# Three paddings in a TensorE-bound two-block kernel: split-precision operands start at a multiple of 256 bytes in place of 64 past it

## The reference

```python
def first_block(x, ...):
    xn = rmsnorm(h, norm1_w)
    qd, kd, vd, qc, kc, vc, gd, gc = split(xn @ w_in)
    o_d = diff_attention(qd, kd, vd, ...)        # 8 heads, two maps, a1 - lam * a2, rmsnorm
    o_c = chunk_attention(qc, kc, vc, rel_bias)  # 8 heads
    merged = sigmoid(gd + b) * (o_d @ w_branch_diff) + sigmoid(gc + b) * (o_c @ w_branch_chunk)
    h = h + merged @ w_out
    h = h + peer(rmsnorm(h, norm2_w), peer_wq, keys, u, v)   # 16,384 one-neuron experts
    return rmsnorm(h, final_norm_w)

def second_block(x, ...):
    x = x + 0.5 * rms_norm(swiglu(rms_norm(x, g1), w_gu1, w_down1), g2)
    x = x + rms_norm(hybrid_mixer(rms_norm(x, g3), ...), g4)  # conv, linear recurrence, window attention
    x = x + 0.5 * rms_norm(swiglu(rms_norm(x, g5), w_gu2, w_down2), g6)
    return x
```

## The kernel before

| tensors | before | after |
|---|---|---|
| `wh`, `wl`, `raw`, `resid` | 128 | 128 |
| `xh`, `xl`, `wb`, `wcol` | 64 | 0 |
| `rt`, `dg`, `ones`, `ident`, `iota`, `nd`, `i1T`, `i2T`, `iota8`, `gT` | 224 | 160 |
| the small ones from `ssq` to `lsg` | 0 to 224 | each 64 lower |
| `odh`, `odl`, `och`, `ocl` | 64 | 0 |
| `y`, `gate`, `oc`, `ah`, `al`, `fh`, `fl`, `oh`, `ol`, `gst`, `one2`, `g2` | 128 | 128 |
| `qkT`, `vd`, `vc`, `rb` | 64 | 64 |

## Time and profile before

### The profile page before, as it was taken

How to read it: one execution, slowest core, us unless ns; L and a number is a source line. 1 busy time by engine, 2 the same in 40 slices (tenths; PEclk the granted TensorE clock), 3 DMA queues, 4 the chain that set the end, 5 groups by cost and what they waited for, 6 DMA issues and landing times.

```text
span 1505.2 us, 26993 instructions
## 1 busy us (share of the span) xinstructions
PE 1484.6 (99%) x10806; PEld 1371.5 (91%) x10806; DVE 1064.7 (71%) x1581; ACT 730.3 (49%) x853; POOL 310.3 (21%) x306
## 2 busy tenths in 40 slices
PE   8999999999999999998999999999999999999998
PEld 8989998999999999997888888888999888899986
DVE  6657676699999999845555555566877577787753
ACT  5366654545454554544444444445444457754441
POOL 3000000011100111126666667760000010000000
PEclk9999999999999999999999999999999999999999
DMA  8643354577666678887888888875555553355552
GB/s 311 203 152 138 129 173 168 185 244 245 230 228 211 216 254 278 285 302 271 290 287 288 289 289 291 290 278 187 191 196 197 195 183 119 131 181 192 190 194 80
DMA packets 56697, 329.76 MB, mean 219 GB/s; under 512 B 7536, under 2 KB 7584, under 8 KB 25232
## 3 DMA queue, kind: packets, MB, share of 16 engines
q1 hardware_dynamic: 36288, 259.01, 50.3%
q0 software_dynamic: 20304, 69.21, 12.6%
HBM read 294.64 MB, written 33.55 MB: 218 GB/s over the span
## 4 chain that ended last, share of the span: by engine, by line
PE 96%; DVE 2%; ACT 1%; issue 1%; DMA 0%; DVEq 0%; ACTq 0%
PE ub L1909 18%; PE ub L1911 17%; PE ub L1910 17%; PE acc L1909 11%; PE acc L1911 11%; PE acc L1910 11%; PE acc L2151 3%; PE acc L2022 1%; PE mb L2046 1%; PE mb L1911 1%; PE mb L1910 1%; PE mb L1909 1%; PE mb L2032 0%; PE acc L2126 0%; DMA resid<-in_x 0%
## 5 line engine op out<-in xcount | busy, mean ns | idle before, releaser
L963 DVE TENSOR_TENSOR wl<-raw,wh 128x2048 fp32r<-128x2048 f32 x244 | 560.3, 2299 | 203.2 <-ACT wh L555 137.9
L1909 PE MATMUL ub<-xh,wh 128*128 128x256 f32 x2168 | 608.8, 281 | 1.7 <-DVE wl L1189 0.8
L1911 PE MATMUL ub<-xh,wl 128*128 128x256 f32 x2168 | 601.0, 277 | 0.0
L1910 PE MATMUL ub<-xl,wh 128*128 128x256 f32 x2168 | 601.0, 277 | 0.0
L1909 PEld LDWEIGHTS ub<-xh,wh 128*128 128x128 f32 x2168 | 407.3, 188 | 10.2 <-issue 6.1
L1910 PEld LDWEIGHTS ub<-xl,wh 128*128 128x128 f32 x2168 | 408.8, 189 | 0.1
L555 ACT CAST wh<-raw 128x2048 fp32r<-128x2048 f32 x184 | 351.0, 1909 | 116.3 <-DMA raw<-in_wstream 116.0
L1911 PEld LDWEIGHTS ub<-xh,wl 128*128 128x128 f32 x2168 | 407.1, 188 | 0.0
L1909 PE MATMUL acc<-wh,ah 128*128 128x512 f32 x512 | 200.6, 392 | 3.9 <-issue 3.9
L1910 PE MATMUL acc<-wl,ah 128*128 128x512 f32 x512 | 200.2, 391 | 0.0
L1911 PE MATMUL acc<-wh,al 128*128 128x512 f32 x512 | 200.1, 391 | 0.0
(11 more groups left out here) (377 smaller groups left out, 1765.2 us busy)
## 6 DMA issues: line engine op xcount, KB each, us to landing
raw<-in_wstream SPq DMA_DIRECT2D x244, 1024.0 KB, 4.9
gates<-gst POOLq DMA_DIRECT2D x16, 1024.0 KB, 14.7
gl_in<-gates POOLq DMA_DIRECT2D x64, 256.0 KB, 3.7
hidden<-hid POOLq DMA_DIRECT2D x60, 256.0 KB, 4.9
hid<-hidden POOLq DMA_DIRECT2D x60, 256.0 KB, 3.6
resid<-in_x SPq DMA_DIRECT2D x2, 512.0 KB, 4.1
rb<-in_rel POOLq DMA_DIRECT2D x1, 1024.0 KB, 6.0
wb<-in_ffn_post_g POOLq DMA_DIRECT2D x2, 512.0 KB, 5.2
```

Of the source, the lines that this page charges most:

```text
L963: v.tensor_tensor(wl[:, slot, :], raw[:, slot, :], wh[:, slot, :].bitcast(F32), ALU.subtract).then_inc(w_low, 1)
L1909: pe.matmul(dst, sh, mh, start=first, stop=False)
L1910: pe.matmul(dst, sh, ml, start=False, stop=False)
L1911: return pe.matmul(dst, sl, mh, start=False, stop=last)
```

## The change

The first unused tensor shrinks by 64 bytes, and the second grows by as much; between the two everything starts 64 bytes lower, and behind the second nothing moves. The third, ahead of `odh`, shrinks by 64 bytes; nothing but `odh`, `odl`, `och` and `ocl` lies behind it on its stack.

```diff
@@ build_program
         resid = sb("resid", [P, TT, D])
-        sb("shift_x", [P, 48])
+        sb("shift_x", [P, 32])
         xh = sb("xh", [P, KD, T], F32R)
         xl = sb("xl", [P, KD, T], F32R)
...
         lsg = sb("lsg", [P, 6, LT])
-        sb("shift_y", [P, 48])
+        sb("shift_y", [P, 64])
...
-        sb("shift_o", [P, 24], at=st2)
+        sb("shift_o", [P, 8], at=st2)
         odh = sb("odh", [P, KD, T], F32R, at=st2)
```

## The result

| | before | after |
|---|---|---|
| median, us | 1506.2 (4 runs, 1503.15 to 1509.45) | 1530.5 (4 runs, 1530.06 to 1531.09) |
| ratio | | 1.0145, 95% interval 1.0123 to 1.0168 |
| span of the traced execution, us | 1505.2 | 1528.9 |

One execution of the kernel before, among 14 in the series beside the first experiments, took 3006.4 us in a slow state and is left out of the ratios.

The account below looks back on a forecast made before the run. TensorE, busy 99% of the span, was taken as the bound: matmul count times spacing. All four terms were taken as 0 on the profiled 1506.85 us, which stands 0.25 us under the median, giving 1507.1 us; range 1499 to 1531 us.

Parts of the forecast that it names:

- the rivals at both ends: Matmul spacing in units: only the short rhythm, 1499.7 us, 15%; the longer one in all units, 1530.3 us, 20%.
- The bound and the readings: TensorE busy 99% of the span; time is matmul count times spacing; chunks with ah, al stationary stay at 226.7 ns.
- Two rhythms, chosen by breaks: 256-column units run at 113.3 or 117.8 ns, a break in the stream choosing; the longer costs 6.8 us now.
- part 1: xh, xl moving at 0 against wh, wl at 128, 6,648 matmuls: taken as 0, bounds -6.8 and +23.2 us.
- Part 2: odh, odl, och, ocl, 288 more matmuls of the same kind: 1.3 us at most, taken as 0.
- Part 3: xh, xl as stationary operands, 288 matmuls at 2.2 ns: between -0.6 and +0.6 us, taken as 0.
- Part 4: ident, dg, rt, wb, wcol and small tensors, mostly hidden behind TensorE: 0.4 us either way, taken as 0.
- the longer rhythm in all units: Rival for the units, L1909 to L1911: every spacing in the longer rhythm, +23.2 us, 1530.3 us; chance 20%.
- only the short rhythm: Rival: at 128 bytes' distance the reads never meet in the costly way, -7.4 us, 1499.7 us; chance 15%.
- The rule weighed: TensorE's moving and weight reads use independent ports, so every term is 0 and the time 1507.1 us.

Follow-up runs that it names:

- rest_only: Against the kernel before: xh and xl stay at 64, all else that the change moved is 64 bytes lower modulo 256; 1508.4 us (10 runs), ratio 1.0019.
- x_at_128: Against the kernel before: xh and xl start at 128 modulo 256, as wh and wl do, all else unmoved; 1534.1 us (4 runs), ratio 1.0166.

## Why the prediction was wrong

The forecast was 1507.1 us, no change; 1530.5 was measured. That this lies inside the stated range of 1499 to 1531 us says little, since the range had been drawn around the rivals at both ends.

- **The bound and the readings** held: 99% busy, the loss is all in spacings, the other engines don't show in it, the chunks without moved operands stayed at 226.7 ns.
- **Two rhythms, chosen by breaks** held at the old distance and is now shown for the breaks by transposes, by moving one and by 16 changes of rhythm in 16. Its size (4.45 ns, 6.8 us in that trace) was right.
- **The step that failed is the choice in part 1** to carry both rhythms over to a distance of 128 bytes, because they occur at 64. No row bore on it, as the text says itself; "most natural" stood in for a row. The runs show that each distance has its own set: at -64 and 64 two rhythms with the short one among them, at 128 and at 0 none at 113.3. The term put at 0 measured +28.8 us (114.47 to 118.91 ns).
- **Part 2** was sized right (up to 1.3 us; 1.3 us measured), its taken value of 0 wrong for the same reason. **Part 3** went over its upper end: 1.0 us for +0.6, 232.4 ns where twice the addition would have been 231.1. **Part 4** isn't contradicted (`rest_only`: ratio 1.0019, at most 1.0040, with 1.3 us of it from part 2), but its 0.4 us is far below what these times can tell.
- **The rival "the longer rhythm in all units"** gave 1530.3 us, and 1530.5 was measured. The agreement is in part luck. The spacing is not the old long one of 117.8 ns but patterns of 118.7 to 120 ns, which make the units 6.9 us dearer than that rival's sum, and 6.8 us are given back where the experts' values begin. I had the 3.9 us wait there and did not ask what slower units would do to it, nor that the clock behind it had fallen.
- **Against the rival "only the short rhythm"** I had said that a load fills the whole time of a 256-column matmul and half of a 512-column one. The profile records 0.19 us for a load of either kind, against spacings of 113.3 and 226.7 ns; that shows a difference between the two, but not "half". Equal starts are free for chunks and the worst of the four for units. That the load is the reason isn't shown: no run changes the width alone.
- **The rule weighed**, from the Trainium skill (TensorE: Matmul & The Clock Gate, section Part 2: What happens when you issue a matmul), independent read ports with no loss to the running matmul, gives 0 for a change of addresses. `x_at_128` is 1.7% slower with the same instructions, so by these runs the stream of matmuls is not indifferent to where the two operands start.

Two line numbers ahead of the prediction are off: `three` begins at L1906 and `acc_chunk` at L1958.

## What to carry to other kernels

Where TensorE is the bound with float32r matmuls of 256 columns and a load before each, the starts of the moving and the stationary operand relative to each other, modulo 256 bytes, can be worth something with not one instruction changed; here it was up to 1.7%. Try the four distances in steps of 64 bytes, keep all operands of a stream at one remainder, and try it anew for another width, since the best distance for 512 columns was the worst of the four for 256. When a kernel that nothing disturbs varies by 0.5% from run to run, look at the spacing of its matmuls stretch by stretch as well as at its waits. And before adding up a slowdown, look for a wait behind it that it will fill, and for the clock behind that wait.

## What was not expected of the hardware

- Seven starts of one operand give steady patterns from 113.3 to 120.0 ns for 256 columns and 226.7 to 233.4 ns for 512.
- A break of three transposes turned one rhythm into the other 16 times out of 16.
- With the high part at 0 and the low part at 64 units took more (120.1 ns in the mean, single spacings of 131) than with both at 0 (118.7).
- After 3.9 us in which TensorE stood still the granted clock over the next 6 us was 0.52, and spacings of 0.43 us in place of 0.23 added 2.8 us.
